# Three sets of rows moved in SBUF: other distances between the rows of x and of the gate, and another place for the inner tile's low part

## What is computed

```
for i in range(2):                                  # block 1
    h = h + 0.5 * swiglu(rmsnorm(h), ffn1_w_gu[i], ffn1_w_down[i])      # inner width 2816
    u = rmsnorm(h) @ w_in[i]                        # convolution, attention, two gates
    merged = sigmoid(g_conv) * y_conv + sigmoid(g_mla) * y_mla
    h = h + merged @ w_o[i]
    h = h + 0.5 * swiglu(rmsnorm(h), ffn2_w_gu[i], ffn2_w_down[i])
    h = h + sigmoid(rmsnorm(h) @ w_ple_gate[i]) * (p[i] @ w_ple_proj[i])
h = rmsnorm(h)
for i in range(2):                                  # block 2
    q, k, v, qi, ki, wi, u_conv, u_pool = split(rmsnorm(h) @ w_in[i])
    mix = concat(sparse_attention, conv, pool) @ w_out[i]
    h = h + rmsnorm(mix)
    m = square(relu(rmsnorm(h) @ w_up[i])) @ w_down[i]                  # inner width 4096
    h = h + rmsnorm(m)
    h = h + sigmoid(h @ ple_gate[i]) * (p[i] @ ple_proj[i])
```

## Time and profile before

| | |
|---|---|
| median of 3 runs | 1979.66 us (1977.69 to 1979.69) |
| span of the profiled execution | 1978.2 us |
| PE, PEld busy | 1935.2 us, 1916.9 us |
| DVE, ACT, POOL busy | 1350.9 us, 996.9 us, 237.4 us |
| matmuls, each with a weight load | 16060 |
| read from HBM | 326.14 MB, 165 GB/s over the span |
| granted TensorE clock | 0.994 of full in the mean |

### The profile page before, as it was taken

One profiled execution on the slowest core, in us unless ns is written; L12 is line 12 of the kernel. 1 busy time (PEld: TensorE's weight loads), 2 busy tenths in 40 slices (PEclk: granted clock), 3 DMA queues, 4 the chain that ended last, 5 costly groups with the idle time before them and its releaser, 6 DMA issues.

```text
span 1978.2 us, 36952 instructions
## 1 busy us (share of the span) xinstructions
PE 1935.2 (98%) x16060; PEld 1916.9 (97%) x16060; DVE 1350.9 (68%) x1608; ACT 996.9 (50%) x1233; POOL 237.4 (12%) x168
## 2 busy tenths in 40 slices
PE   8999999999999999999999999998999999899999
PEld 8999999999999999999999999898999999799998
DVE  6655777775559655687785557896855589676556
ACT  5443545563437444545554445776533466654443
POOL 3000100010002000100010001473100016710000
PEclk9999999999999999999999999999999999899999
DMA  8555454465554655544556554424555543237551
GB/s 278 199 180 182 144 174 160 133 211 192 192 183 156 213 182 183 183 137 143 171 171 213 185 181 152 158 67 132 170 187 187 166 152 113 70 112 231 191 183 53
DMA packets 246533, 329.57 MB, mean 167 GB/s; under 512 B 6246, under 2 KB 218788, under 8 KB 246372
## 3 DMA queue, kind: packets, MB, share of 16 engines
q1 hardware_dynamic: 246018, 326.79, 50.0%
q0 software_dynamic: 96, 0.26, 0.1%
q10 hardware_dynamic: 258, 0.16, 0.0%
HBM read 326.14 MB, written 1.05 MB: 165 GB/s over the span
## 4 chain that ended last, share of the span: by engine, by line
PE 79%; DVE 12%; POOL 3%; ACT 3%; DMA 1%; issue 1%; SPq 0%; POOLq 0%; DVEq 0%; ACTq 0%
PE work L2028 17%; PE work L2029 17%; PE work L2030 17%; PE acc L2028 9%; PE acc L2030 9%; PE acc L2029 9%; DVE w_lo L1313 4%; POOL fa L747 2%; ACT w_hi L800 1%; DVE ra L1326 1%; DMA raw<-in_w_in_dram 1%; DVE xl L1347 1%; DVE fa L1358 1%; POOL fa L741 1%; PE acc L2105 1%
## 5 line engine op out<-in xcount | busy, mean ns | idle before, releaser
L1313 DVE TENSOR_TENSOR w_lo<-raw,w_hi 128x2048 fp32r<-128x2048 f32 (+2 forms) x313 | 709.8, 2271 | 107.8 <-ACT w_hi L800 105.8
L2028 PE MATMUL work<-xh,w_hi 128*128 128x256 f32 x2560 | 721.8, 282 | 9.6 <-DVE w_lo L1313 6.1
L2029 PE MATMUL work<-xl,w_hi 128*128 128x256 f32 x2560 | 718.6, 281 | 0.0
L2030 PE MATMUL work<-xh,w_lo 128*128 128x256 f32 x2560 | 717.0, 280 | 0.0
L800 ACT ACTIVATE w_hi<-raw 128x2048 fp32r<-128x2048 f32 (+2 forms) x313 | 576.6, 1849 | 165.4 <-PE work L2030 74.6
L2028 PEld LDWEIGHTS work<-xh,w_hi 128*128 128x128 f32 x2560 | 482.3, 188 | 13.9 <-issue 8.0
L2029 PEld LDWEIGHTS work<-xl,w_hi 128*128 128x128 f32 x2560 | 483.0, 189 | 0.3
L2030 PEld LDWEIGHTS work<-xh,w_lo 128*128 128x128 f32 x2560 | 483.1, 189 | 0.0
L2028 PE MATMUL acc<-ra,w_hi 128*128 128x256 f32 x1352 | 380.1, 281 | 0.0
L2030 PE MATMUL acc<-ra,w_lo 128*128 128x256 f32 x1352 | 379.7, 281 | 0.0
L2029 PE MATMUL acc<-ra,w_hi 128*128 128x256 f32 x1352 | 378.9, 280 | 0.0
(11 more groups left out here) (302 smaller groups left out, 2324.7 us busy)
## 6 DMA issues: line engine op xcount, KB each, us to landing
raw<-in_ffn_w_gu_dram SPq DMA_DIRECT2D x88, 1024.0 KB, 5.1
raw<-in_w_in_dram SPq DMA_DIRECT2D x52, 1024.0 KB, 5.5
raw<-in_ffn_w_down_dram SPq DMA_DIRECT2D x44, 1024.0 KB, 4.9
raw<-in_w_up_dram SPq DMA_DIRECT2D x32, 1024.0 KB, 5.3
raw<-in_w_down_dram SPq DMA_DIRECT2D x32, 1024.0 KB, 4.9
raw<-in_w_mla_out_dram SPq DMA_DIRECT2D x8, 1024.0 KB, 5.5
raw<-in_w_o_dram SPq DMA_DIRECT2D x8, 1024.0 KB, 4.9
raw<-in_w_ple_gate_dram SPq DMA_DIRECT2D x8, 1024.0 KB, 5.0
```

The costliest lines, as they stand in the source:

```text
L1313: v.tensor_tensor(w_lo[:, s, 0:n], raw[:, r, 0:n], w_hi[:, s, 0:n].bitcast(F32), ALU.subtract).then_inc(lo_done.sem, 1)
L2028: pe.matmul(dst, ah, bh, start=start and i == 0, stop=False, skip_group_check=not group)
L2029: pe.matmul(dst, ah, bl, start=False, stop=False, skip_group_check=not group)
L2030: last = pe.matmul(dst, al, bh, start=False, stop=stop and i == len(pairs) - 1, skip_group_check=not group)
```

## The change

It adds no instruction, no wait and no transfer, and only moves rows. `xh` and `xl` become two cuts of one allocation of the same size (4160 floats), with rows 258 floats (1032 bytes) apart and the low part 2064 floats (8256 bytes) behind. The rows of the gate come to lie 262 floats (1048 bytes) apart, its low part 2096 floats (8384 bytes) behind the high part. The inner tile keeps its 1040 bytes, but its low part goes from 4160 to 4352 bytes behind the high part. The allocations behind these keep their addresses.

```
-ROW = T + 4
+X_SIZE, X_ROW, X_AT = 4160, 258, (0, 2064)
+H_ROW, H_AT = 260, (0, 1088)
+G_ROW, G_AT = 262, (4160, 6256)
...
-        xh = sb("xh", [P, KD, ROW], F32R)[:, :, 0:T]
-        xl = sb("xl", [P, KD, ROW], F32R)[:, :, 0:T]
+        x_rows = sb("x_rows", [P, X_SIZE], F32R)
...
+        def rows_at(arena, at, n, row):
+
+            return cut(arena, at, n, row)[:, :, 0:T]
+
+        xh, xl = (rows_at(x_rows, at, KD, X_ROW) for at in X_AT)
...
-        hh, hl = (cut(ra, i * 4 * ROW, 2, 2, ROW)[:, :, :, 0:T] for i in range(2))
+        hh, hl = (rows_at(ra, at, 4, H_ROW).rearrange("p (a b) t -> p a b t", a=2) for at in H_AT)
...
-        gh, gl = (cut(ra, 4 * ROW * 4 + i * KD * ROW, KD, ROW)[:, :, 0:T] for i in range(2))
+        gh, gl = (rows_at(ra, at, KD, G_ROW) for at in G_AT)
```

## The result

The changed kernel takes 1984.31 us (median of 8 runs) against 1979.43 us for the kernel before: a ratio of 1.0025, with an interval of 1.0016 to 1.0034. That is 4.9 us slower. The forecast was 1968.4 us, faster than before.

The account below looks back on a forecast made before the run. TensorE was taken to bound the kernel by the distance of its matmul starts. Span 1978.2 less 3.4 (inner tile) and 7.9 (x and gate) is 1966.9, plus 1.5 to the median: 1968.4 us; range 1954 to 1989.

Parts of the forecast that it names:

- What bounds the kernel: Whole kernel: TensorE, busy in 98% of 1978.2 us, sets the time by the distance of its matmul starts.
- Nearly one for one: Whole kernel: what moves the distance of TensorE's matmul starts moves the end by nearly as much.
- The inner tile: 76 down chunks of 48 matmuls: offset 64 to 0 brings x's pace, 5.675 to 5.63 us each, 3.4 us less.
- The target of 5.63: Time in us of one x unit of 48 matmuls, 117.3 ns each, which the down chunks were expected to reach.
- The rival of the 120.0 ns pace: Inner tile's high and low parts in step, as in w_o's stretch: 6.5 us more, 1986.2 us; chance 0.13.
- x and gate: 8832 matmuls on x and gate rows: steps of 8 and 24 bytes gain 0.9 ns each, 7.9 us less.
- one common position against steps of 16 bytes: w_o's stretch, rows all alike, at 120.0 ns a matmul against an x unit, rows stepping by 16 bytes, at 117.3.
- the 2.7 ns: Claimed worth of row position per matmul, from w_o's stretch at 120.0 ns against the x unit at 117.3.
- The rival off the grid: Odd x and gate rows off the 16-byte grid cost 1.9 ns on 4416 matmuls: 8.4 us more, 1988.1 us; chance 0.15.
- The sum: Whole kernel: span 1978.2 - 3.4 - 7.9 = 1966.9 us, with the median 1.5 us above it, 1968.4 us.

## Why the prediction was wrong

- **What bounds the kernel** was right. Only the distance of matmul starts moved, the unmoved rows kept 5761 ns, and no other engine changed. "Nearly one for one" was too strong: of 7.6 us more in TensorE's busy time the waits gave back 3.9 in the trace.
- **The inner tile**: forecast 3.4 us less, measured 3.3 in the trace and 3.9 by medians with that part alone (1979.49 to 1975.56). Right in sign and size, and the size with some luck. Its reason, that an offset nearer to 0 brings x's pace, is only in part borne out: 5629 and 5664 at offset 128, 5653 and 5618 at 192. With offset 0 and every distance kept, but the whole tile 16 or 128 bytes further on, the gain over before shrinks from some 47 ns a chunk to 21 and 14. The target of 5.63 was one unit's, 9 ns under the median unit of 5640. The rival of the 120.0 ns pace, 5761, didn't come.
- **x and gate**: this step failed, in its sign. A gain of 7.9 us was taken (0.9 ns a matmul), and the trace shows a loss of 9.3: 8.3 on x's starts and 1.0 on the gate's, 1.0 and 1.3 ns a matmul (the median x unit lost more, 1.4). The error was to read the pace of a new step from one comparison, one common position against steps of 16 bytes, and to carry a third of it on to positions of another kind. The rows of before had no operand off the grid, and the text said so: they priced no such row, so the sign was a guess. The comparison itself doesn't hold either: in the two runs with enlarged weight tiles w_o's rows kept all their distances, and took 117.7 ns instead of 120.0. So the 2.7 ns were not the price of a common position as such.
- **The rival off the grid** had the right sign for x and gate and nearly the right size, 8.4 against 9.3 us. Its mechanism, one fetch more for a row off the grid, is refuted by place 12, so the agreement in size is luck. The sign that was named for it, an x unit at 5.70 us or above, came (5.71), but it tells the loss and not the mechanism. For the gate the loss is the pitch's, as it is there at all three offsets tried: 71, 65 and 77 ns. For x the same pitch costs 31 ns at offset 128 and none at 0, and the low part's move to offset 64 costs another 35; x at offset 64 on the grid was not tried, since it doesn't fit the allocation. So about half of x's loss comes only with pitch and low part's position together, and no rule was found for it. Whether the distance of the parts or the low part's own position matters isn't shown: sets moved as a whole on the grid changed by up to 54 ns with every distance kept.
- **The sum**: with the inner tile as forecast and the rival's price for x and gate, 1978.2 - 3.4 + 8.4 is 1983.2 of span, against 1981.9. The range took that rival with no gain beside it, and its upper end of 1989 held the time.

What sets the pace at the four places stays open. A load still begins 2 to 5 ns behind the start of the matmul before it, as in the earlier trace rows, and its own matmul starts later: 110 to 119 ns after the load's start in a unit of before, 115 to 123 with x at place 4. That place counts relative to the weights was excluded, the count of lines as the only cause too.

## What to carry to other kernels

When TensorE streams float32 rows at the pace of its weight loads, where the rows begin in SBUF was worth up to 5 ns of a 118 ns matmul here (5586 to 5824 ns for the same 48), and it is read from one unit's first start to the next unit's. Measure each tile's layout in its own stretch, several tiles in one run, and sum; once the units had been measured, the sums held within 2 us here. Keep the rows that stream away from 4 and 8 bytes past a multiple of 16, expect tens of ns on 48 matmuls from a move on the grid too, and don't extend a trend in placement beyond the kind of position that was measured.

## What was not expected of the hardware

- Rows of 256 float32 that begin 4 bytes past a multiple of 16 cost 201 to 221 ns on 48 matmuls, at 8 bytes 96 to 166, at 12 bytes they cost 6 for x and gain 18 to 37 for the others.
- The cost of place 4 follows the operand that streams: weights that stream took 121.6 ns a matmul at place 4 and 118.1 at place 0, rows of x that are stationary 118.8 at place 4.
- With each weight tile enlarged by 32 bytes, all later allocations moved with it, and w_o's input, whose rows weren't moved within their arena, went from 5761 to 5651 ns, from 120.0 to 117.7 ns a matmul. The place of the weights as stationary operand is not the reason: it is 5653 with them at 4.

```profile
401.29 0.28 PE L2035 MATMUL work<-ra,w_hi 128*128 128x256 f32 x1
...
406.94 0.27 PE L2182 MATMUL work<-consts,vrow 128*128 128x128 f32 x1
```

  That stretch, here with the weights at place 0, had been 120.0 in every other layout. Which of the moves did it, the low weights' or the arena's, wasn't separated.
